# Attention in a diffusion block: values stationary in column halves, softmax sums spread by TensorE, head-pair loop written out

## The reference

```
def context_attention(q, k, v):            # 2 blocks of 128 queries per head, 256 keys
    s = einsum(q, k) * scale
    return einsum(softmax(s), v)

def neighbourhood_attention(q, k, v, k_ctx, v_ctx, rpb):   # 8 blocks of 8 x 16 queries per head
    s_lat = einsum(qb, kg) * scale + bias  # 12 x 32 = 384 keys around the block, masked
    s_ctx = einsum(qb, k_ctx) * scale      # 512 cached keys
    p = softmax(concatenate([s_lat, s_ctx]))
    return einsum(p[:384], vg) + einsum(p[384:], v_ctx)
```

## Time and profile before

| | |
|---|---|
| median of 3 runs | 3747.21 us (3743.26 to 3751.91) |
| profiled execution, its own time | 3747.23 us |
| its span in the trace | 3745.6 us |
| PE busy | 3515.9 us, 94% |
| DVE busy | 2199.0 us, 59% |
| ACT busy | 1695.7 us, 45% |
| attention, first transposes of values to first product of the output projection | 1055.4 to 1612.4 us of the span |

### The profile page before, as it was taken

The page is one execution under the profiler, slowest core; times in us unless marked ns, Lnnn a source line. Parts: engine busy times, 40 slices in busy tenths (PEclk is TensorE's granted clock), DMA queues, the critical chain, the costliest instruction groups (busy, mean ns, idle before and its releaser), DMA issues. The chain is left out here.

```text
span 3745.6 us, 57442 instructions
## 1 busy us (share of the span) xinstructions
PE 3515.9 (94%) x22128; PEld 2881.1 (77%) x22128; DVE 2199.0 (59%) x3714; ACT 1695.7 (45%) x2430; POOL 651.0 (17%) x517
## 2 busy tenths in 40 slices
PE   5899999999989999999999589999999999999991
PEld 3799999999988888888887566676666766667671
DVE  5745554545456666632222666666666666666673
ACT  3611111111157777621110566666666666666662
POOL 0000000000064646201010101111111111211210
PEclk7899999999999999999999799999999999999996
DMA  9543444343465646464642668888888888888886
GB/s 375 178 139 130 131 134 135 126 140 118 143 204 164 191 144 200 151 240 147 229 139 86 272 254 295 294 295 295 294 295 295 294 294 294 296 295 295 295 281 249
DMA packets 381005, 826.63 MB, mean 221 GB/s; under 512 B 27392, under 2 KB 167072, under 8 KB 353184
## 3 DMA queue, kind: packets, MB, share of 16 engines
q1 hardware_dynamic: 355232, 702.28, 53.6%
q0 software_dynamic: 25600, 121.93, 10.0%
HBM read 717.18 MB, written 108.00 MB: 220 GB/s over the span
## 5 line engine op out<-in xcount | busy, mean ns | idle before, releaser
L2207 DVE TENSOR_TENSOR e_wlo<-e_raw,e_whi 128x1024 fp32r<-128x1024 f32 x512 | 599.3, 1221 | 70.6 <-ACT e_whi L2138 62.6
L2138 ACT ACTIVATE e_whi<-e_raw 128x1024 fp32r<-128x1024 f32 x512 | 509.3, 1051 | 118.6 <-PE ps L2343 76.2
L2343 PE MATMUL ps<-e_whi,e_xhi 128*128 128x512 f32 x1024 | 413.3, 404 | 1.0 <-DVE e_wlo L2207 1.0
L2343 PE MATMUL ps<-e_wlo,e_xhi 128*128 128x512 f32 x1024 | 399.7, 390 | 0.0
L2343 PE MATMUL ps<-e_whi,e_xlo 128*128 128x512 f32 x1024 | 398.6, 389 | 0.0
L549 PE MATMUL ps<-hhi,p_whi 128*128 128x428 f32 (+1 forms) x1536 | 381.6, 357 | 8.4 <-DVE p_wlo L481 8.4
L499 DVE SCALAR_TENSOR_TENSOR p_acc<-p_modraw,cT,p_acc 128x256 f32<-128x256 f32 x960 | 386.5, 479 | 0.5 <-DMA p_modraw<-in_w_mod 0.5
L549 PE MATMUL ps<-hlo,p_whi 128*128 128x428 f32 (+1 forms) x1536 | 381.9, 357 | 0.0
L549 PE MATMUL ps<-hhi,p_wlo 128*128 128x428 f32 (+1 forms) x1536 | 380.1, 356 | 0.0
L2096 POOL TENSOR_TENSOR e_carried<-ident 128x1 f32<-128x1 f32 x31 | 179.5, 5792 | 1097.8 <-DVE e_ys L2240 1096.5
L2207 DVE TENSOR_TENSOR e_wlo<-e_raw_third,e_whi 128x1024 fp32r<-128x1024 f32 x256 | 297.4, 1220 | 87.8 <-ACT e_whi L2138 86.3
(11 more groups left out here) (266 smaller groups left out, 5968.2 us busy)
## 6 DMA issues: line engine op xcount, KB each, us to landing
e_raw<-in_w_gate SPq DMA_DIRECT2D x96, 1024.0 KB, 5.2
e_raw<-in_w_up SPq DMA_DIRECT2D x96, 1024.0 KB, 7.6
p_modraw<-in_w_mod SPq DMA_DIRECT2D x128, 512.0 KB, 3.5
e_raw_third<-in_w_down SPq DMA_DIRECT2D x64, 1024.0 KB, 7.1
e_raw<-in_w_down SPq DMA_DIRECT2D x64, 1024.0 KB, 6.6
m_raw<-in_w_mod SPq DMA_DIRECT2D x16, 2048.0 KB, 13.2
p_raw<-in_w_in SPq DMA_DIRECT2D x64, 512.0 KB, 4.7
o_raw<-in_w_out SPq DMA_DIRECT2D x16, 2048.0 KB, 9.3
```

Source lines behind the costliest of these rows:

```text
L2138: nc.scalar.activation(whi[:, c % 2, f], raws[c % RAWS][:, f], ACT.Copy).then_inc(w_hi_made, 1)
L2207: nc.vector.tensor_tensor(wlo[:, c % 2, f], raws[c % RAWS][:, f], whi[:, c % 2, f].bitcast(F32), ALU.subtract).then_inc(w_lo_made, 1)
L2343: last = nc.tensor.matmul(ps[:, bank, :], x, w[:, c % 2, f], start=(k == 0 and i == 0), stop=(k == of - 1 and i == 2))
```

## The change

`values` now handles two query blocks of one head at once, in odd steps only. The head's 64 value columns of a key tile are the stationary operand and the 128 transposed probabilities the moving one. The first block (even unit) is written to partitions 0 to 63 of bank 6 and the second to partitions 64 to 127, and the matmuls of the two alternate. The result is already turned (features on partitions), so the transposes of `a_pairs`, `pair_high`, `split_pair` and `turn_last_pair` go. What has to be spread over features is the inverse of each query's sum: in even units `turn` adds, for either half, a matmul with the inverse broadcast over 64 columns as stationary operand and the identity as moving one, into the spare 128 columns that `copy_turned` copies. `output` is now one multiplication per two blocks, bank 6 by the copied inverses, into `att`; `head_high` and `head_low` split a whole head. `ORDER` puts the eight latent blocks first and the two context blocks last, `prT` has three slots, `pr` keeps four. SP stores a pair's rows with eight DMAs, in the course of the next body instead of at the end of its own, and issues the pooling transfers before them. The loop over `j` is written out on every engine.

```
-    ORDER = [(True, 0), (True, 1), (True, 2), (True, 3), (False, 0), (True, 4), ... (True, 7), (False, 1)]
+    ORDER = [(True, b) for b in range(LW)] + [(False, b) for b in range(CB)]
+    PW_HEAD = W // 2
+    HALF_LAT, HALF_CTX = LAT // 2, CTX // 2
+    HTOK = HALF_LAT + HALF_CTX
+    PRTS = 3
...
 (SP)
-            sp.wait_ge(out_lo, j * W + W + AHEAD)
-            for dst, src in ((v["mixhi_d"], athi), (v["mixlo_d"], atlo)):
-                sp.dma_start(dst[ds(j * P, P), :], src[:].bitcast(F32)).then_inc(att_stored, 16)
             if not last:
-                load_cached_values(j + 1, 1)
                 if pool_store:
                     store_pool(j - 1)
                 load_pool(j, j + 2)
+                sp.wait_ge(valued, j * W + W)
+                load_cached_values(j + 1, 1)
+            sp.wait_ge(out_lo, j * 2 + 2)
+            for h in range(2):
+                for dst, src in ((v["mixhi_d"], athi), (v["mixlo_d"], atlo)):
+                    dest, mine = dst[j * P + h * DH:...], head_tokens(src, h).bitcast(F32)
+                    for part, cols in ((dest[:, 0:LAT], mine[:, 0:HALF_LAT]), (dest[:, LAT:TOK], mine[:, HALF_LAT:HTOK])):
+                        sp.dma_start(part.rearrange("f (a t) -> a f t", a=2), cols).then_inc(att_stored, 16)
...
 (ACT, copy_turned)
+            g = j * U + u
+            act.wait_ge(turned, g + 1 + AHEAD)
+            if g >= PRTS:
+                act.wait_ge(valued, (g - PRTS) // 2 + 1)
+            if g % 2 == 0 and g >= 2 * PRTS + 2:
+                act.wait_ge(out_scaled, g // 2 - PRTS)
...
+        def head_high(j, h):
+            act.wait_ge(out_scaled, j * W + (h + 1) * PW_HEAD)
+            act.wait_ge(att_stored, j * 128 + AHEAD)
+            nc.scalar.activation(head_tokens(athi, h), att[:, h, :], ACT.Copy).then_inc(out_hi, 1)
...
 (ACT, body)
-                if pair_with(u + 1) is not None:
-                    pair_high(j, pair_with(u + 1))
+                if u == 1 and j:
+                    head_high(j - 1, 1)
+                if u == W + 1:
+                    head_high(j, 0)
...
 (DVE)
+        def inverses(q):
+            s = st[:, 2 * q % 4:2 * q % 4 + 2, :]
+            dve.wait_ge(exped, 2 * q + 2)
+            if q >= 2:
+                dve.wait_ge(turned, 2 * q - 1 + AHEAD)
+            nc.vector.reciprocal(s[:, :, 4], s[:, :, 3]).then_inc(inverted, 1)
+        def output(q):
+            h, w = divmod(2 * q % U, W)
+            dve.wait_ge(copied, 2 * q + 3)
+            dve.wait_ge(valued, q + 1)
+            nc.vector.tensor_tensor(block_of(att[:, h, :], w), as_block(ps[:, 6, 0:P], w),
+                                    as_block(prT[:, (2 * q + 2) % PRTS, NKEY:1024], w), ALU.mult).then_inc(out_scaled, 1)
...
 (DVE, body)
-                output(j, u)
+                if u % 2 == 0:
+                    inverses((j * U + u) // 2)
+                    if j or u:
+                        output((j * U + u) // 2 - 1)
...
 (PE, turn)
-            w = pair_with(u)
-            if w is not None:
-                pe.wait_ge(out_scaled, j * U + (W + w + 1) + AHEAD)
-                last = nc.tensor.transpose(ps[:, 5, 512 - P:512], pairs[:, w, :], ident[:])
+            if g and g % 2 == 0:
+                pe.wait_ge(inverted, g // 2)
+                for half in range(2):
+                    f = slice(half * DH, half * DH + DH)
+                    last = nc.tensor.matmul(ps[f, 5, 512 - P:512],
+                                            st[:, (g - 2 + half) % 4, 4:5].broadcast_to([P, DH]), ident[:],
+                                            start=True, stop=True)
...
 (PE, values)
-            pe.wait_ge(out_scaled, j * U + u + AHEAD)
-            for c, t in enumerate(tiles):
-                last = nc.tensor.matmul(ps[:, 6, 0:DH], prT[:, u % 2, c * P:c * P + P], t, ...)
+            if g > 1:
+                pe.wait_ge(out_scaled, g // 2)
+            n = 3 + PAST // P if latent else CB
+            for c in range(n):
+                for half in range(2):
+                    slot = prT[:, (g - 1 + half) % PRTS, c * P:c * P + P]
+                    if not latent:
+                        t = Vx[:, c, f]
+                    else:
+                        t = V[:, b // 2, half + c, f] if c < 3 else vc[:, c - 3, f]
+                    last = nc.tensor.matmul(ps[half * DH:half * DH + DH, 6, 0:P], t, slot, ...)
...
-            with pe.Fori(1, J - 1) as j:
-                body(j, True)
+            for j in range(J):
+                body(j, j > 0, j == J - 1)
```

More of the change, by code:

```diff
@@ L1075, in following_bodies @@
             copy_turned(0, 0)
-            body(0, False)
-            with act.Fori(1, J - 1) as j:
-                body(j, True)
-            body(J - 1, True, True)
-            act.wait_ge(out_lo, J * W + AHEAD)
+            for j in range(J):
+                body(j, j > 0, j == J - 1)
+            head_high(J - 1, 1)
+            act.wait_ge(out_lo, J * 2)
             projection()
@@ L1156, in body @@
                     pool_low(j, LAST_POOL_AT[u - 1])
-                if pair_with(u + 1) is not None:
-                    split_pair(j, pair_with(u + 1))
+                if u == 2 and j:
+                    head_low(j - 1, 1)
+                if u == W + 2:
+                    head_low(j, 0)
                 if u == 2:
@@ L1175, in following_bodies @@
                 stats(0, u)
-            body(0, False)
-            with dve.Fori(1, J - 1) as j:
-                body(j, True)
-            body(J - 1, True, True)
-            dve.wait_ge(att_stored, 32 * J + AHEAD)
+            for j in range(J):
+                body(j, j > 0, j == J - 1)
+            output(J * W - 1)
+            head_low(J - 1, 1)
+            dve.wait_ge(att_stored, 128 * J + AHEAD)
             dve.wait_ge(pooled_stored, 32 * NPOOL + AHEAD)
@@ L1239, in values @@
-            pe.wait_ge(out_scaled, j * U + u + AHEAD)
-            for c, t in enumerate(tiles):
-                last = nc.tensor.matmul(ps[:, 6, 0:DH], prT[:, u % 2, c * P:c * P + P], t,
-                                        start=(c == 0), stop=(c == len(tiles) - 1))
+            pe.wait_ge(copied, g + 1)
+            if g > 1:
[4 more added lines that the diff above has]
+                    slot = prT[:, (g - 1 + half) % PRTS, c * P:c * P + P]
+                    if not latent:
+                        t = Vx[:, c, f]
+                    else:
+                        t = V[:, b // 2, half + c, f] if c < 3 else vc[:, c - 3, f]
+                    last = nc.tensor.matmul(ps[half * DH:half * DH + DH, 6, 0:P], t, slot, start=(c == 0),
+                                            stop=(c == n - 1))
@@ L1243, in values @@
             last.then_inc(valued, 1)
-        def turn_last_pair(j):
-            pe.wait_ge(copied, j * U + (U + 1))
-            pe.wait_ge(out_scaled, j * U + U + AHEAD)
-            nc.tensor.transpose(ps[:, 5, 512 - P:512], pairs[:, W - 1, :], ident[:]).then_inc(pair_turned, 1)
         def project_pool(n, t):
@@ L1289, in body @@
                     project_pool(j, LAST_POOL_AT[u])
-            turn_last_pair(j)
         def following_bodies():
@@ L1302, in following_bodies @@
             turn(0, 0)
-            body(0, False)
-            with pe.Fori(1, J - 1) as j:
-                body(j, True)
-            body(J - 1, True, True)
-            out.tensor(pe, ((pair_copied, J + AHEAD), (out_scaled, J * U + AHEAD), (pooled_lo, 3 * NPOOL + AHEAD)))
+            for j in range(J):
+                body(j, j > 0, j == J - 1)
+            out.tensor(pe, ((copied, J * U + 1), (out_scaled, J * W), (pooled_lo, 3 * NPOOL + AHEAD)))
         return following_bodies
```

134 lines of the change are left out of this document (44 added, 90 removed).

## The result

The changed kernel takes 3885.89 us (median of 4 runs, 3883.29 to 3887.54), the kernel before on the same chip 3749.31 us (4 runs, 3743.26 to 3751.91). The ratio is 1.0363, with a 95% interval of 1.035 to 1.0375. I had forecast 3690 us in a range of 3655 to 3722, so the time lies outside the range and on the other side of no change.

A forecast was written before the change was run, and what follows sets the result against it. The prediction took the PE to bound attention, 62 of 65.5 us per head pair. Terms of -7.8, -2.4 and +3.2 gave -7.0 us a pair, times 8 = -56, from 3747.2 to 3690 us, range 3655 to 3722.

The forecast's parts named there:

- the one on SP: SP's queue per head pair: eight stores issue in 4.4 us, vT issued at 14 us; cost 0, bound 3 us.
- The end of the stage: After the last head pair: store to next load about 12 us, covered by 23.8 us of products, so 0.
- The values: PE value products: two halves run at once, 0.053 us a record, saving 11.8 and 0.9 us a pair.
- the rival without overlap: Column halves in the PE's value products do not overlap: 0.107 us a record, 3793 us; chance 0.07.
- The change of mode: PE entering and leaving column halves: 0.3 us a round trip, thirteen trips, adding 3.9 us a pair.
- the sum: All terms for one head pair in attention: -7.8 work, -2.4 waits gone, +3.2 waits come, -7.0 us.
- Waits that come: PE waiting in steps without value products to cover ACT's round trip: 0.25 to 0.6 us each, +3.2 a pair.
- ACT's round trip takes over: Latent steps in attention last about 3.0 us, giving 3710 us; chance 0.17 for ACT or SP taking half.
- The inverses: PE matmuls spreading inverse sums: ten times four records at 0.053 us, adding 2.1 us a pair.
- Writing out the loops: Removing register steps and branches of the head-pair loop: a gain of 0.2 us a pair.

The follow-up runs named there:

- Experiment 1: The changed kernel with each of a head pair's eight stores cut into two of 64 partitions; 3733.12 us.
- Experiment 3: The kernel before, its two stores per head pair replaced by eight of the change's 2 x 64 x columns shape; 3967.78 us, ratio 1.0582.
- 13: The changed kernel with its large stores cut by columns, twelve per head pair, outer dimension of 2 kept; 3894.17 us.
- experiment 5: Experiment 1 with SP's list reordered: vT's load first, then the previous head 1's stores, head 0's stores in the middle of its own body; 3697.78 us.
- experiment 9: Experiment 5's SP order, but with the change's eight stores of 2 x 64 x columns; 3767.66 us.
- experiment 14: Experiment 9 with each head's four stores moved behind the loads of the next keys and queries; 3782.01 us.
- Experiment 12: The changed kernel with only the last head pair's stores cut in two of 64 partitions; 3865.35 us.
- experiment 2: Experiment 1 with all value matmuls of the first column half, then all of the second, instead of alternating; 3764.31 us.
- Experiment 7: Experiment 1 with value products split: key tiles 0 to 3 in the odd step, 4 to 6 in the following even step; 3735.35 us.
- experiment 10: Experiment 5 without the matmuls spreading the inverse sums, except in the first and last couple; output scaled by a stale inverse; 3688.82 us.
- experiment 4: The kernel before with its loop over head pairs written out on all four engines, nothing else; 3754.62 us, ratio 1.0015.
- 8: Experiment 1 with SP's new order, DVE's reciprocal first, value products cut in two and ACT's long copies one or two steps later; 3695.7 us.
- 11: Experiment 5 with DVE's reciprocal first and ACT's long copies two steps later, value products not cut; 3693.46 us.

## Why the prediction was wrong

**The step that failed** is the one on SP. The prediction says that the eight stores "take some 4.4 us to issue (0.38 for one and a gap, eight times, an estimate)", and takes SP as 0 with a bound of 3 us a pair. I priced the issue of a new pattern with the row of an old one. The store before has 128 rows as its outer dimension; the new one was written as 2 x 64 x columns. It measured 21.4 us, and with the issue of `vT` behind it 29.3. The forecast had `vT` issued at 14 us into the body, landed between 18 and 22 and needed at about 19, but its issue ended 29.3 us behind the first store, near 39 us into the body, and ACT waited up to 26.1 us for it. The bound of 3 us wasn't a bound, since nothing in the trace of before showed the new pattern.

**The size of this step.** Experiment 1 takes it out alone: 3885.9 to 3733.1, 152.8 us. Between the two profiled executions it is 149.7, 130.5 of them in attention (669.5 to 539.0 us) and 19 behind it. Experiment 3 puts it alone into the kernel before: +218.7. Experiments 1 and 13 differ in the outer dimension at the same or nearly the same size (161 us). In the Trainium skill, DMA: Bandwidth & Descriptors, section "Why a DMA increments its semaphore by 16 and not by 1", is a rule that fits: the number of DMA engines that a transfer is spread over is the largest, up to 16, that divides the slowest dimension of both patterns, so 2 x 64 x 512 is given two. The trace agrees, with a DMA share of 0.13 to 0.14 (2 of 16 is 0.125) and two packets in flight at once, and with 0.52 and up to sixteen where the outer dimension is 64. How long a transfer on two engines holds the issuing queue, the trace alone shows: some 6.5 us for two stores of 320 KB together, about 50 GB/s.

**The place of the stores on SP** is a second part of it. With wide stores SP was still held 10.1 us, more than the 4.4 expected, and `vT` and `kraw` were waited for 13.1 and 28.2 us. Putting `vT` first and parting the sixteen stores, eight ahead of either head's next queries and keys (experiment 5), gave 35.3 us. Width and place aren't independent: a narrow store in the good order costs 70 us (experiment 9), and one moved further back holds back the buffer that it reads (experiment 14). A store of one head that holds its queue for 10.7 us (one case of experiment 9) to 16.5 (one of experiment 14) and its buffer until it lands has found no place in these two orders where nobody waits for one of them.

**The end of the stage.** "now about 12", taken as 0 under a cover of 23.8 us, was 31.0. Experiment 12 prices it at 20.5 us. The step's form was right, cover less wait, and the same wrong issue time broke it.

**What held.** The values: 0.054 us a record for the 0.053 taken, so the rival without overlap is out; experiment 2 shows a pitch of 0.11 within one half, and costs 31 us, less than its 73 us of longer values since waits took part of them up. The change of mode: 0.26 to 0.30 us a round trip for the 0.3 taken, by the single starts in the trace of the change. Around the values (15 places, medians) it is 0.09 ahead of them, 0.15 within and 0.02 behind; around four inverses between transposes (22 places) 0.09, 0.15 and 0.06. Experiment 7 bears it out in kind, where eight more round trips per pair ate the gain. With SP's stores widened and put behind the loads (experiment 5) a head pair takes 61.2 us (the loads of `vT` in the rows below are five pairs apart) for 66.5 before (332.5 us over the same five), 5.3 less where the sum said 7.0, and attention 509.5 us for 557.0, 47.5 less for 56; the whole time of 3697.8 us lies 8 from the forecast and inside its range.

```profile
1143.53 0.33 SPq L784 DMA_DIRECT2D vT<-projT  x1
...
1449.65 0.33 SPq L784 DMA_DIRECT2D vT<-projT  x1
```

**What was off in size.** *Waits that come* was 3.2 us a pair. In experiment 5 the PE waits 31.2 us for ACT's copies in 430 us, 4.4 in a pair of 61.2 us; a single one was up to 1.4 and not 0.25 to 0.6. They lie between my forecast and the rival "ACT's round trip takes over" (3710). *The inverses* were 1.1 for 2.1 us a pair (experiment 10). *Writing out the loops* was to give 0.2 us a pair and costs about 5.6 us in the kernel before (experiment 4). Over eight pairs these three are +10 (1.2 x 8), -8 (1.0 x 8) and +7 (5.6 and the 1.6 counted as a gain), together +9, close to the 8 us that are left. That sum is arithmetic from experiments on three different kernels and not shown.

**What stays open.** Why the written-out loop is slower. And what bounds experiments 5, 8 and 11, within 4.3 us of each other though each has other waits of the PE: PE, DVE and ACT wait for each other in turn, and taking a part of one wait away didn't shorten the ring.

## What to carry to other kernels

When a change gives a transfer a new pattern, price it from a row with that pattern, or take it as unknown: one whose outer dimension is 2 can be slower than two whose outer dimension is 64, and it holds every DMA behind it on its queue. Write the bound of a queue's cost by the bytes over the slowest rate that could be, and not by the issue time of a neighbour. And read a wait on an engine one step further: here "PE waits for ACT" was ACT waiting for a load that stood behind a store.

## What the runs showed of the hardware

- Stores of 2 x 64 x columns ran at a DMA share of 0.13 to 0.14 and about 50 GB/s. The first two were issued in 1.1 us, the following ones held the queue for some 6.5 us per two, and the load behind them for 7.9.
- Idle time costs twice. In 1339.80:1347.60 the PE ran nothing and its granted clock was 0.52, next to the 1.2 GHz level; over attention it was 0.86, for 0.98 in experiment 5. For nearly the same instructions the PE was busy 474.6 us there and 450.5 here, so some 24 of the 160 us between the two stages are slower work, not waiting. The trace bears it out: the PE was busy 64.6 us at the lower level in this stage and 12.8 in experiment 5, and half of the difference is 26. In the pair of the stretches above the clock was low from 1340.1 to 1360.6; the PE had run nothing since 1335.9 when it fell, and was at work again from 1355.3.
- Two column halves that use the same 128 rows, in alternating records, ran at 0.054 us a record, half the pitch of one half (0.11). The Trainium skill, TensorE: Matmul & The Clock Gate, Part 3, The mechanism, lets a weight load overlap running matmuls only where row groups differ; the measurement decides against it for this case.
- The PE took records of the second half ahead of their place when the first half's stood in a row (experiment 2), but only three or four: with fourteen in a row eleven ran alone, at 0.11 us, and with four in a row none did.
- A change between full width and column halves and back cost 0.26 to 0.30 us of start-to-start time, around four records as around 28.
